# More expert weights cast beforehand, weight loads on another engine's queue, and expert rows moved in steps of 32

## What is computed

```python
h = _modulate(_rmsnorm(x, norm1_g), shift1, scale1)
q, k, v, p, gl = split(h @ w_in)              # w_in: 1024 x 5632
o = _rmsnorm(_diff_attention(q, k, v, lam), subln_g) * (1 - lambda_init)
attn_out = o @ w_br_attn
pool_out = _pool_mixer(p, pool_w, pool_scale) @ w_br_pool
merged = g[0] * attn_out + g[1] * pool_out    # g = sigmoid(gl + b_gate)
x = x + gate1 * (merged @ w_out)
h2 = _modulate(_rmsnorm(x, norm2_g), shift2, scale2)
# _hier_moe(h2): every row goes to 2 of 16 experts
gates = ...                                   # (T, 16), two of them not zero
a, u = t @ expert_w_gate[e], t @ expert_w_up[e]      # 1024 x 512 each
out = sum_e (silu(a) * u * gates[:, e]) @ expert_w_down[e]   # 512 x 1024
x = x + gate2 * out
```

## Time and profile before

| | us |
|---|---|
| median of 3 runs | 1667.09 (1658.35 to 1671.49) |
| the profiled execution | 1662.04 |
| its span on the slowest core (7) | 1660.5 |
| spans of the 8 cores | 1627.4 to 1660.5 |
| busy on core 7: PE, DVE, ACT, POOL | 1117.8, 658.6, 635.7, 530.1 |

### The profile page before, as it was taken

The page is one execution under the profiler, slowest core; times in us unless marked ns, Lnnn a source line. Parts: engine busy times, 40 slices in busy tenths (PEclk is TensorE's granted clock), DMA queues, the critical chain, the costliest instruction groups (busy, mean ns, idle before and its releaser), DMA issues.

```text
span 1660.5 us, 24636 instructions; the slowest of 8 cores (1627.4 to 1660.5 us)
## 1 busy us (share of the span) xinstructions
PE 1117.8 (67%) x7785; PEld 608.5 (37%) x7785; DVE 658.6 (40%) x1448; ACT 635.7 (38%) x1036; POOL 530.1 (32%) x424
## 2 busy tenths in 40 slices
PE   0386684457986246767678789699634677868575
PEld 0232231233443123332345455344213345545343
DVE  0343234541233558841313332223453344545344
ACT  1244423762222243332578788122312223323221
POOL 2043210323344567741102220333542212233132
PEclk9999797658997669988788899799857788989888
DMA  9957699981662783516699696362959999997994
GB/s 214 152 77 117 128 145 38 256 250 69 89 102 77 178 166 53 75 19 96 85 104 118 90 104 91 126 89 45 207 123 240 212 248 248 273 234 150 184 173 81
DMA packets 126010, 229.28 MB, mean 138 GB/s; under 512 B 16964, under 2 KB 76356, under 8 KB 120200
## 3 DMA queue, kind: packets, MB, share of 16 engines
q0 software_dynamic: 87584, 129.10, 55.0%
q1 hardware_dynamic: 38248, 97.99, 20.7%
HBM read 261.75 MB, written 89.28 MB: 211 GB/s over the span
## 4 chain that ended last, share of the span: by engine, by line
PE 45%; DMA 17%; DVE 13%; issue 9%; ACT 7%; POOL 5%; another core or an unknown queue 1%; DVEq 1%; SPq 1%; POOLq 0%; ACTq 0%
PE psall L130 28%; DMA hT<-h2slot 8%; PE psall L128 7%; PE psall L1260 4%; DVE PL L153 3%; PE psall L133 3%; DVE ACC L153 3%; DMA ring<-w_ada 3%; POOL ACC L153 3%; DMA y<-cpkb,effi 3%; PE psall L1286 2%; ACT PL L150 2%; DVE KR L163 1%; DMA y<-PL,effi 1%
## 5 line engine op out<-in xcount | busy, mean ns | idle before, releaser
L150 ACT ACTIVATE PL<-psall 128x1024 bf16<-128x1024 f32 x224 | 213.7, 1059 | 31.4 <-PE psall L130 31.3
L130 PE MATMUL psall<-ring,hT 128*128 128x512 bf16 x768 | 194.4, 408 | 0.0
L128 PE MATMUL psall<-X,PL 128*128 128x129 bf16 x1792 | 162.5, 239 | 44.3 <-DVE ACC L163 34.1
L130 PE MATMUL psall<-hT,ring 128*128 128x512 bf16 x640 | 158.9, 405 | 0.0
L128 PEld LDWEIGHTS psall<-X,PL 128*128 128x128 bf16 x1792 | 115.8, 105 | 102.3 <-issue 98.6
L1297 POOL DMA_INDIRECT y<-PL,effi x44 | 65.7, 1493 | 194.7 <-DVE PL L1292 109.9
L130 PE MATMUL psall<-ACC,KR 64*128 64x256 bf16 x896 | 99.4, 302 | 28.1 <-issue 15.4
L130 PEld LDWEIGHTS psall<-ring,hT 128*128 128x128 bf16 x768 | 77.1, 104 | 87.7 <-issue 19.9
L153 DVE TENSOR_TENSOR PL<-psall,PL 128x512 f32<-128x512 f32 x64 | 44.3, 692 | 161.2 <-PE psall L130 141.5
L130 PEld LDWEIGHTS psall<-hT,ring 128*128 128x128 bf16 x640 | 66.3, 104 | 86.0 <-issue 20.7
L150 ACT ACTIVATE PL<-psall,cpkb 128x512 bf16<-128x512 f32 x64 | 43.9, 689 | 139.7 <-PE psall L130 139.7
(11 more groups left out here) (189 smaller groups left out, 2032.6 us busy)
## 6 DMA issues: line engine op xcount, KB each, us to landing
h2slot<-xst SPq DMA_DIRECT2D x16, 1040.0 KB, 19.7
hT<-h2slot SPq DMA_DIRECT2D x64, 260.0 KB
X<-x SPq DMA_DIRECT2D x32, 512.0 KB, 7.9
ring<-w_in POOLq DMA_DIRECT2D x14, 1024.0 KB, 13.0
ring<-w_ada POOLq DMA_DIRECT2D x12, 1024.0 KB, 26.6
ring<-w_in POOLq DMA_DIRECT2D x16, 512.0 KB, 13.3
y<-X SPq DMA_DIRECT2D x16, 512.0 KB, 4.8
ewb<-ew_gate POOLq DMA_DIRECT2D x8, 1024.0 KB, 13.3
```

Source lines behind the costliest of these rows:

```text
L128: return self.add('pe', lambda e: e.matmul(out, lhsT, rhs, start=start, stop=stop, skip_group_check=True), [lhsT, rhs], [out])
L130: return self.add('pe', lambda e: e.matmul(out, lhsT, rhs, start=start, stop=stop), [lhsT, rhs], [out])
L150: return self.add('act', lambda e: e.activation(out, in_, func, **kw), ins, outs)
```

## The change

Three things are changed together.

1. All of the experts 2 to 15 are cast to `ewb` beforehand: 42 `conv` DMAs instead of 24. Seven stand in pass 0's merging (one at the end of each `blk` but the last), 4 in pass 1's pooling, 28 in its attention (one every 7 steps), 3 in its merging. `ewb` now holds an expert's three matrices side by side in one row of 24,576 bytes.
2. The weights of experts 2 to 15 are loaded by `L_bf` on ACT's queue, with one or two DMAs per expert; no weights are cast in `moe`.
3. Slot rows are fetched and results scattered in steps of 32 rows: every `hs_load` and every scatter has its own branch over 4 or 5 sizes (`rows`). So SP reads all 17 registers, and POOL clears the six-number tails of the seven row buffers first; the mask `vldm` is applied to the target rows.

```diff
-    ewb = dscr("ewb", [8, 3, 128, 4096], BF16)
+    ewb = dscr("ewb", [14, 128, 12288], BF16)
@@
-                if en != 'sp':
-                    S.load_regs(en, ['c%d' % i for i in range(16)] + ['nov'], cnti, cnti[0:1, 0:17])
-            S.load_regs('sp', ['nov'], cnti[:, 16:17], cnti[0:1, 16:17])
+                S.load_regs(en, ['c%d' % i for i in range(16)] + ['nov'], cnti, cnti[0:1, 0:17])
@@ out_norm2
         if p == 1:
-            L_static(0)
-            L_static(1)
+            for i in range(NDIR):
+                for m in range(3):
+                    L_cast(i, m)
@@
-                if p == 1:
-                    L_static(2)
             if 0 <= s_ - 1 < 8:
                 TR(s_ - 1)
+            if p == 1 and s_ == 8:
+                L_bf(2)
@@ at_A
-            if p == 1 and n % 9 == 2 and convs:
+            if p == 1 and n % 7 == 2 and convs:
@@ merging, after the two column blocks of blk
+                if convs and (2 * ng + blk < 7 or p == 1):
+                    conv(*convs.pop(0), after=[ix])
@@
+    NDIR = 2
-        dst = ewb[i - NB, m]
+        dst = ewb[i - NDIR, :, m * 4096:(m + 1) * 4096]
+    convs = [(i, m) for i in range(NDIR, 16) for m in range(3)]
@@
+    def L_bf(i):
         b = i % NB
+        kin = [('ewb', i, m_) for m_ in range(3)]
+        for k, (dst, c0) in enumerate(EWF[b]):
+            n = dst.shape[1]
+            S.dma('act', dst, ewb[i - NDIR, :, c0:c0 + n], ('eh', b, k), kin=kin)
@@ moe
+        def rows(s, j):
+            b0 = 128 * j
+            if j == 0:
+                return ('exp', 'c%d' % s.e, (32, 64, 96)), (32, 64, 96, 128)
+            return ('exp', 'c%d' % s.e, (b0, b0 + 32, b0 + 64, b0 + 96)), (8, 32, 64, 96, 128)
@@ hs_load
-                ix = S.dma('sp', HI[b], h2slot[r0:r0 + 128, :], ('hs', b), kin=h2keys)
+                S.region, ns = rows(s, j)
+                S.add('sp', [(lambda e, n=n, b=b, r0=r0: e.dma_start(out=HI[b][0:n, :], in_=h2slot[r0:r0 + n, :])) for n in ns],
+                      (), [HI[b]], h2keys, dma=('hs', b))
+                S.region = None
@@ D_: the scatter
-                vary('pool', mks, j, 128, 8, [effi[:, sc:sc + 1], yb], (), s.ykin, [s.ykout[j]], dma=('ys', s.tag, s.ys[j]))
+                keep, ns = S.region, (128,)
+                if s.main:
+                    S.region, ns = rows(s, j)
+                S.add('pool', [mks(n) for n in ns], [effi[:, sc:sc + 1], yb], (), s.ykin, [s.ykout[j]],
+                      dma=('ys', s.tag, s.ys[j]))
@@
+        for b in range(7):
+            S.memset('pool', HX[b], 0.0)
-        ix = hs_load(srcs[0])
+        hs_load(srcs[0])
...
-        L_static(3, [ix])
-        LATE = {0: [(4, 0), (4, 1)], 1: [(4, 2)]}
+        L_bf(3)
+        L_bf(4)
@@ end of expert i
-            if i + NB < 13:
-                L_static(i + NB)
-            for i2, m in LATE.get(i, []):
-                L_cast(i2, m)
+            if i + NB < 16:
+                L_bf(i + NB)
```

More of the change, by code:

```diff
@@ L464, in build_program @@
     dmy = A("dmy", [128, 64], F32)
+    vldm = A("vldm", [128, 64], F32)
     effi = A("effi", [128, 8], I32)
@@ L710, in router @@
                  bc(dtab[:, 64:68], [128, 16, 4]), ALU.is_le)
+            S.ts('dve', vldm[:], dmy[:], -1.0, -1.0, ALU.mult, ALU.subtract)
             S.tt('dve', dmy[:], dmy[:], dtab[:, 0:64], ALU.mult)
@@ L944, in rg @@
             return v3(buf)[:, :, 8 + a: 8 + b]
-        convs = [(i, m) for i in range(NB, 13) for m in range(3)]
         (up,), upj = W.acquire()
@@ L1118, in run_pass @@
                     S.tt('dve', t0s[s2], PS[b0 + 2][:, 0:512], sg0[s2], ALU.mult)
-                    S.tt('pool', mrgT[:, c, tsl], t0s[s2], t1s[s2], ALU.add)
+                    ix = S.tt('pool', mrgT[:, c, tsl], t0s[s2], t1s[s2], ALU.add)
+                if convs and (2 * ng + blk < 7 or p == 1):
+                    conv(*convs.pop(0), after=[ix])
             W.release(ugj)
@@ L1131, in build_program @@
           [KR[:, m * 4096:(m + 1) * 4096] for m in range(3)]]
+    EWF = [[(ringflat[:, 4096:16384], 0)], [(accb[:, 0:8192], 0), (mixf, 8192)],
+           [(accb[:, 8192:16384], 0), (ringflat[:, 16384:20480], 8192)], [(X1b_[:, 0:12288], 0)], [(KR[:], 0)]]
     NB = 5
@@ L1156, in L_cast @@
         S.add('pool', lambda e_: e_.dma_start(out=dst, in_=src), (), [dst], dma=('ew', b, m), after=after)
-    def L_static(i, after=()):
+    def L_bf(i):
         b = i % NB
-        for m in range(3):
-            if i >= NB:
-                S.dma('sp', EW[b][m], ewb[i - NB, m], ('eh', b, m), kin=[('ewb', i, m_) for m_ in range(3)])
-            else:
-                L_cast(i, m, after)
+        kin = [('ewb', i, m_) for m_ in range(3)]
+        for k, (dst, c0) in enumerate(EWF[b]):
+            n = dst.shape[1]
+            S.dma('act', dst, ewb[i - NDIR, :, c0:c0 + n], ('eh', b, k), kin=kin)
     def moe():
@@ L1205, in main_src @@
             s.dm = [dmy[:, 4 * e + j:4 * e + j + 1] for j in range(4)]
+            s.valid = [vldm[:, 4 * e + j:4 * e + j + 1] for j in range(4)]
             s.eid = float(e)
@@ L1213, in main_src @@
             return s
+        def rows(s, j):
[3 more added lines that the diff above has]
+            return ('exp', 'c%d' % s.e, (b0, b0 + 32, b0 + 64, b0 + 96)), (8, 32, 64, 96, 128)
         def hs_load(s):
-            ix = None
             for j in range(4):
@@ L1219, in hs_load @@
                 r0 = s.e * 2048 + j * 128
-                ix = S.dma('sp', HI[b], h2slot[r0:r0 + 128, :], ('hs', b), kin=h2keys)
-            return ix
+                S.region, ns = rows(s, j)
+                S.add('sp', [(lambda e, n=n, b=b, r0=r0: e.dma_start(out=HI[b][0:n, :], in_=h2slot[r0:r0 + n, :])) for n in ns],
+                      (), [HI[b]], h2keys, dma=('hs', b))
+                S.region = None
         def T1(s, j, bank=4):
@@ L1235, in extras @@
                 eo, wo = effi[:, sc:sc + 1], wcol[:, sc:sc + 1]
-                if s.main:
-                    S.tt('dve', eo, hx[:, 0:1], s.dm[j], ALU.add)
-                else:
-                    S.stt(eo, hx[:, 0:1], s.valid[j], s.dm[j], ALU.mult, ALU.add)
+                S.stt(eo, hx[:, 0:1], s.valid[j], s.dm[j], ALU.mult, ALU.add)
                 S.ts('dve', wo, hx[:, 4:5], s.eid, hx[:, 2:3], ALU.is_equal, ALU.mult)
@@ L1299, in mks @@
                         in_=yb[0:n, :], in_offset=None, compute_op=ALU.add)
-                vary('pool', mks, j, 128, 8, [effi[:, sc:sc + 1], yb], (), s.ykin, [s.ykout[j]], dma=('ys', s.tag, s.ys[j]))
+                keep, ns = S.region, (128,)
[3 more added lines that the diff above has]
+                      dma=('ys', s.tag, s.ys[j]))
+                S.region = keep
         srcs = [main_src(i) for i in range(16)]
-        ix = hs_load(srcs[0])
+        for b in range(7):
+            S.memset('pool', HX[b], 0.0)
+        hs_load(srcs[0])
         for j in range(4):
@@ L1307, in moe @@
         hs_load(srcs[1])
-        L_static(3, [ix])
-        LATE = {0: [(4, 0), (4, 1)], 1: [(4, 2)]}
-        for i in range(13, 16):
-            for m in range(3):
-                LATE.setdefault(i - NB + m, []).append((i, m))
+        L_bf(3)
+        L_bf(4)
         for i in range(16):
@@ L1451, in build_program @@
     moe()
+    assert not convs
     S.emit()
```

## The result

The changed kernel takes 1676.34 us (median of 20 runs) against 1658.43 us for the kernel before (median of 20 runs beside them). The ratio is 1.0087, with a 95% interval of 1.0057 to 1.0118: 0.9% slower, where 3.3% faster had been forecast and 1590 us to 1650 us given as the range. The ratio leaves out the executions that fell in a slower state of the chip, and so it isn't the quotient of the two medians. The profiled execution took 1662.06 us, the shortest of the 20 and as long as the one profiled before (1662.04): the two traces show where time went, but not the 0.9%.

The account below looks back on a forecast made before the run. PE was taken to bound pass 0's merging, the DMA engines the experts' stage. Core 4: 1655.9 + 6 (start) + 5 (pass 0) - 62 (experts' stage) = 1605, (1605 + 1.5) x 1.003 = 1611 us; range 1590 to 1650.

Parts of the forecast that it names:

- What bounds the kernel: PE limits pass 0's merging; DMA engines, busy for 0.93, bind the experts' stage, their work there falling to 255 to 268 us.
- (c): Pass 1: 32 casts and one refill just fill the 274 us stage; cost taken as 0, up to 15 us.
- the stage: Core 4's experts' stage: 309 us plus 8 for what remains late, 317 instead of 379, 62 us less.
- The forecast's sum for core 4: Core 4's whole run: 1655.9 + 6 + 5 - 62 = 1605 us.
- (b): Pass 0's merging: seven casts, two ahead of each `ng`'s refills, make ring weights late; 5 us, 0 to 15.
- casts don't fit: Rival: at 11 us per cast, refills queue behind casts and PE stands in both mergings; 94 us more, 1705; chance 0.07.
- (a): Start of the experts' stage: SP's first fetch waits for POOL's register reads and clearings; 6 us later, 0 to 11.
- landings stay late: Rival: in the experts' stage scatters still land late beside large loads; adds 30 us, about 1641; chance 0.15.
- The rival that it frees nothing: Experts' stage: token rows wait for the engines' total load, not SP's queue; 36.8 us remain, 1648; chance 0.08.
- (d): Experts' stage: four branches per expert on SP and four on POOL instead of one; cost taken as 0.

Follow-up runs that it names:

- e2_layout: The changed kernel with each stored matrix contiguous and three weight loads per expert; ratio 1.0002 to the kernel before.
- e12_fewatt: The changed kernel with 22 casts in attention, 1 in pass 1's merging and eight in pass 0's `out_norm2`; ratio 0.9994 to the kernel before.
- e8_gap: The changed kernel with contiguous matrices, casts spread outside the mergings, and stored weights loaded after the next expert's third chain; ratio 0.9688 to the kernel before.
- e5_split: The changed kernel, wide rows kept, with each expert's weights loaded in three DMAs of 8 KB pieces; ratio 0.9982 to the kernel before.
- e10_aftgap: The changed kernel with only an expert's stored weights loaded later, after the third chain of the next expert; ratio 0.9927 to the kernel before.
- e3_steps: The kernel before with the steps of 32 rows alone; ratio 0.9791 to the kernel before.

## Why the prediction was wrong

**What bounds the kernel: right.** In the experts' stage the DMA engines were busy for 0.72 of 351.6 us on core 4, 253 us, where 255 to 268 had been forecast; the row waits between experts vanished, and the stage became shorter, by 27 us and 48 us. Two terms failed: (c), taken as 0, and the stage, taken as 317 us. Neither turns the sign alone. The forecast's sum for core 4, 1605, with the 28 us of (c) or the 35 us of the stage is 1633 or 1640, both below the 1655.9 before; together they are above it.

**(b), pass 0: mis-sized.** 5 us was taken, 10.1 us and 9.8 us measured on cores 4 and 5 (w_out), inside the 0 to 15 given. The DMA share came to 0.77 on core 7 and 0.83 on core 4, not near 1.

**(c), pass 1: the step that failed first of all.** "Just full", with a backlog of some 20 us crossing into the merging, was taken as 0. The wait was 28 us on core 4, 35.7 on core 7, 37.9 on core 5, and attention itself stayed as long as before, as forecast. Two things were wrong in it. First the price: 8.3 us per cast came from a stretch with a share of 0.78. Where the queue has no pause it is higher. The casting queue on core 7 from 870 to 1040, before and then after:

```profile
q0 software_dynamic: 3528, 16.53, 77.1%
```

```profile
q0 software_dynamic: 4743, 18.56, 99.4%
```

That is 170 x 0.771 / 16.53 = 7.9 us per MB before and 9.1 after, 9.5 us for one matrix instead of 8.3. The last 24 casts before the merging were issued 8.6 us apart, from 850.15 to 1046.88; the queue moved less than one in that time. e2_layout has 18.50 MB in 100.9% there, so the contiguous layout gives no better price; I had named the rows of 8 KB as the risk, and for the price they are not it. With the contiguous matrices the same casts lengthened attention by some 35 us instead of holding up the refills. Second the cover: I set a refill's 24 us from issue to need beside a backlog of 20 us, but the casts issued around attention's end took 54 us to 81 us to land, and the refill 58. With 22 casts in attention instead of 28 (e12_fewatt, which also has two fewer in the merging) the wait was gone.

**The rival "casts don't fit" came true in part.** It had the right mechanism and place, but its threshold of 10 us per cast was too high: at 9.5 the 32 casts need 304 us in a stage of 274, and the 30 us over met refills without slack. Its 94 us were far too much; PE stood for 38 us on core 4 and 48 us on core 5. It had a chance of 0.07.

**(a), the start: 2 us less instead of 6 more.** POOL on core 5, from its last slot scatter to the clearings, and SP's first fetch (compare):

```profile
1296.33 0.96 POOL L690 DMA_INDIRECT h2slot<-KR,s12i  x1 [0.27 <-issue]
1298.04 0.10 POOL L177 MEMSET hT<- 128x8 f32 x1 [0.74 <-issue]
```

```profile
1300.74 4.72 SPq L1235 DMA_DIRECT2D hT<-h2slot  x6
```

The 17 register reads lie within 0.74 us of idle time, so the 11.69 us in the earlier trace rows were not they but the wait that the row names, for ScalarE's first copy of token rows, which itself stood behind their landing. The fetch came 3.4 us after the last scatter's end, on core 7 too (1290.28 to 1293.70), before 5.5 us there (1251.48 + 0.97 to 1257.96).

**The stage, 317 us forecast for core 4: 351.6.** The DMA sum held, as said above, and the time was lost nevertheless. From the first matmul of each expert to that of the next, PE's timeline of core 4 gives:

| blocks | taken | after, mean | e8_gap, mean |
|---|---|---|---|
| 4 (three experts) | 24.4 | 23.3 | 22.9 |
| 3 (four) | 18.7 | 19.9 | 18.7 |
| 2, behind one of four (three) | 17.9 | 23.9 | 23.3 |
| 2, the other six | 17.9 | 21.8 | 18.1 |

So the clean prices were right for all but one kind, and 18 us come from a term that I didn't have: behind an expert of four blocks, the next one of two takes 5 us to 6 us more even in e8_gap, where little else is late. There PE waits for DVE's first product. Core 4 of the change, a long expert ends at 1373, PE and then DVE:

```profile
1373.11 3.66 PE L1273 MATMUL psall<-ring,KR 128*128 128x256 bf16 x32
...
1384.93 1.86 PE L1273 MATMUL psall<-ring,KR 128*128 128x256 bf16 x8 [6.78 <-DVE xst L1278]
```

```profile
1376.47 0.15 DVE L174 COPY pfc<-hT 128x1 f32<-128x1 f32 x1
1384.36 0.42 DVE L1278 TENSOR_TENSOR xst<-psall,xn 128x256 bf16<-128x256 f32 x1 [7.74 <-issue]
```

DVE has no work left of the long expert: it has finished at 1376.62 and stands idle for 7.74 us, and the profile names nothing that it waits for. The same stands at the two other places (6.73 and 8.91 us), in e8_gap (6.73, 6.02 and 10.13) and in the kernel before (6.75, 6.20 and 13.90), whose experts there take 21.8, 21.2 and 28.8 us. All stand before DVE's first product of the expert behind the long one; before other first products core 4 of the change shows two more (7.25 and 5.07 us). No experiment touched this, so its cause is open.

The other 23 us stand in the six other experts of two blocks, and are for the most part landings of scatters behind weight loads, the rival "landings stay late", which I had priced at 30 for the whole stage: 8 were taken. Three experiments agree on it (e5_split -16 us, e10_aftgap -29 us, e8_gap -30 us on this core); in e10_aftgap these six take 17.2 us at the mean instead of 21.8. The expert from 1422.65 to 1449.11, 26.5 us, shows one: PE, then DVE.

```profile
1422.65 3.65 PE L1273 MATMUL psall<-ring,ACC 128*128 128x256 bf16 x32 [0.60 <-issue]
...
1441.93 2.29 PE L1299 MATMUL psall<-mixT,xst 128*128 128x512 bf16 x5 [5.97 <-DVE PL L1262]
```

```profile
1428.69 0.41 DVE L1278 TENSOR_TENSOR xst<-psall,xn 128x256 bf16<-128x256 f32 x1
1441.19 0.22 DVE L1262 SCALAR_TENSOR_TENSOR PL<-g1b,pfc,g2b 128x2 f32<-128x2 f32 x1 [12.08 <-DMA y<-PL,effi]
```

```profile
1422.24 0.33 ACTq L183 DMA_DIRECT2D ring<-ewb  x1
```

POOL issues the scatter of the tile that DVE wants at 1420.90, ACT one load of 3 MB 1.3 us later (1422.24), and DVE stands for the scatter's landing until 1441.19, 20 us after its issue. e10_aftgap moved this load, and nothing else here.

**The other queue.** The rival that it frees nothing had 0.08. The row waits did go, so as a mechanism it was wrong; as a time it was right (0.9992 for the part alone). The Trainium skill's page "DMA: Bandwidth & Descriptors", section "Issuing engines are not separate DMA queues", states that DMAs started by the scalar, sync or gpsimd engine run on the same 16 engines and interleave. The runs agree as far as they go: 36 us of row waits went on core 7, and DVE's waits for the landings of all output tiles grew by 35 us there and by 42 us on core 4.

**The branches (d): no cost seen.** e3_steps has them all and gains 2.1%; no run prices them alone.

**The sum, corrected** (core 4, one execution): 1655.9, +10.1 and +28.0 for ring weights, -27.0 in the stage make 1667; 1657.3 was measured. The 10 us between are within the 20 us that the start differs by between like executions.

## What to carry to other kernels

A queue that is busy for three quarters has no quarter to give away: its price per job rises as the pauses go, and everything that shares the queue waits for the whole backlog, long after the stage that filled it. So price added transfers at the saturated rate, and look for the first small transfer behind them that somebody waits for; if the transfers are then moved, look for the next one. Large plain loads are best issued a few microseconds after the small transfers that others wait for, and in several DMAs of smaller pieces (here 1.6 and 1.0 points). Two kernels with the same ratio can lose their time at different places, as e2_layout and e5_split do. Test the parts of such a change one by one: the steps of 32 rows alone gave 2.1%, and with spread casts and late loads 3.1%.

## What the runs showed of the hardware that was not expected

- The casting queue's price was 7.9 us per MB at a share of 0.77 and 9.1 us per MB at 0.99, with the wide rows as the target; with contiguous matrices it was 9.3 at 1.01.
- With that queue full, attention took 223 us to 232 us with the wide rows (the change, e5_split) and 259 us to 261 us with contiguous matrices; much of the difference is idle time of PE for which the profile names no releaser.
- With load pieces of up to 24 KB per partition on one queue, indirect scatters on another took at least 12.9 us to land on core 4 and 10.5 on core 7; with three DMAs in pieces of 8 KB, from 8.3 and 6.5 us.
- Loads on SP's own queue landed after 39.8 us at the median beside eight casts on the other, after 6.1 us without them: separate queues did not shield them.
- Seventeen register reads on POOL fit into 0.74 us. The seven clearings took 0.1 us or less each, though on core 5 they lie spread over 2.2 us.
